# Two transformer blocks on one core: the second block's last 128 tokens begin with their convolutions, the head norms are summed as columns, and the chores are paced by the busier engine

## The reference, cut to what matters

```
x = first_block(...)    # adaLN, sparse attention + short convolution, then a product-key expert layer:
                        #   per token 128 experts; each expert's row of 2048 numbers (u, v) is gathered:
                        #   out = sum_e gelu(x . u_e) * g_e * v_e ;  x + gate * out, final rmsnorm
h = rmsnorm(x);  proj = h @ w_in            # w_in: 1024 x 10256
q_a k_a v_a z_a q_b k_b v_b z_b beta decay gate_a gate_b = split(proj)
o_a = causal attention(rope(q_a), rope(k_a), v_a);   y_a = (o_a * silu(z_a)) @ w_branch_a
q_b k_b v_b = silu(causal conv of 4 taps over tokens)
q_b = q_b * rsqrt(sum_head q_b^2 + eps) * dk^-0.5;   k_b = k_b * rsqrt(sum_head k_b^2 + eps)
o_b = gated delta rule(q_b, k_b, v_b, decay, beta)   # state carried from token to token, 8 heads of 128
y_b = (rmsnorm(o_b) * silu(z_b)) @ w_branch_b
out = (sigmoid(gate_a) * y_a + sigmoid(gate_b) * y_b) @ w_out;   return x + rmsnorm(out)
```

## Time and profile before

| what | us |
|---|---|
| median of 3 runs | 1382.6 (1382.16 to 1389.08) |
| the profiled execution, its own time | 1377.14 |
| its span, first to last instruction | 1375.3 |
| TensorE busy | 1099.7 (80%) |
| VectorE busy | 816.1 (59%) |
| ScalarE busy | 450.3 (33%) |
| GpSimd busy | 288.9 (21%) |
| gathers issued | 213.2 to 1040.1 |
| last accumulate | 1057.2 |

### The profile page before, as it was taken

The page is one execution under the profiler, slowest core; times in us unless marked ns, Lnnn a source line. Parts: engine busy times, 40 slices in busy tenths (PEclk is TensorE's granted clock), DMA queues, the critical chain, the costliest instruction groups (busy, mean ns, idle before and its releaser), DMA issues.

```text
span 1375.3 us, 14070 instructions
## 1 busy us (share of the span) xinstructions
PE 1099.7 (80%) x5130; PEld 545.3 (40%) x5130; DVE 816.1 (59%) x1849; ACT 450.3 (33%) x1246; POOL 288.9 (21%) x261
## 2 busy tenths in 40 slices
PE   6989995877786666678877799875888798798687
PEld 2877672432252222123333343323333354454353
DVE  5475656887946998463456765566553317535531
ACT  1121223555433344352334433433342213113111
POOL 0000002434343535433222232331321000000000
PEclk9987977999998999999999899998989899899798
DMA  9995507999999999999999799997988475156132
GB/s 392 328 388 198 199 0 274 336 353 395 383 384 422 420 405 391 422 421 422 420 422 403 270 420 421 421 421 287 421 331 346 180 276 214 66 212 259 76 123 76
DMA packets 63664, 433.14 MB, mean 315 GB/s; under 512 B 6979, under 2 KB 10348, under 8 KB 11884
## 3 DMA queue, kind: packets, MB, share of 16 engines
q0 software_dynamic: 36864, 268.45, 48.4%
q1 hardware_dynamic: 26064, 161.76, 30.0%
q10 hardware_dynamic: 668, 2.04, 0.4%
HBM read 431.17 MB, written 1.06 MB: 314 GB/s over the span
## 4 chain that ended last, share of the span: by engine, by line
PE 44%; DVE 25%; DMA 21%; ACT 7%; issue 3%; POOL 1%; ACTq 0%; SPq 0%; DVEq 0%; POOLq 0%
DMA AR<-in_puv,idx 18%; PE ps L1055 17%; PE ps L1010 8%; DVE AR L1619 8%; PE ps L704 4%; PE ps L1161 2%; PE ps L926 2%; DMA W<-in_w_mod 2%; PE ps L1036 1%; DVE rowb L1766 1%; PE ps L954 1%; DVE tok L1802 1%; DVE rowb L1802 1%; DMA X<-in_x 1%; ACT av L2128 1%
## 5 line engine op out<-in xcount | busy, mean ns | idle before, releaser
L2377 POOL DMA_INDIRECT AR<-in_puv,idx x256 | 288.5, 1127 | 752.7 <-PE ps L1010 501.5
L1010 PE MATMUL ps<-AR,acc 128*64 128x512 f32 x912 | 288.3, 668 | 124.8 <-ACT acc L2011 123.9
L1619 DVE CUSTOM_DVE_ANT_0 AR<-AR,mixT 128x1024 f32<-128x1024 f32 x128 | 153.3, 1222 | 84.2 <-DMA AR<-in_puv,idx 83.9
L1055 PE MATMUL ps<-W,AR 128*128 128x512 f32 x416 | 197.2, 614 | 3.2 <-ACT AR L2011 2.2
L1010 PEld LDWEIGHTS ps<-AR,acc 128*64 128x64 f32 x912 | 72.2, 146 | 293.3 <-ACT acc L2011 201.5
L1619 DVE CUSTOM_DVE_ANT_0 AR<-AR,tok 128x1024 f32<-128x1024 f32 x128 | 153.2, 1220 | 58.6 <-DMA AR<-in_puv,idx 58.5
L2126 ACT ACTIVATE av<-av 128x1 f32<-128x1 f32 x256 | 51.6, 201 | 353.1 <-DVE av L1619 352.8
L1055 PE MATMUL ps<-W,hT 128*128 128x512 f32 x320 | 155.1, 616 | 6.0 <-ACT rowb L2011 6.0
L1055 PEld LDWEIGHTS ps<-W,AR 128*128 128x128 f32 x416 | 77.6, 197 | 81.5 <-issue 76.0
L1055 PEld LDWEIGHTS ps<-W,hT 128*128 128x128 f32 x320 | 57.5, 194 | 85.5 <-issue 76.8
L704 PE MATMUL ps<-hT,W 128*128 128x256 f32 x320 | 76.8, 403 | 8.7 <-DVE AR L1343 6.1
(11 more groups left out here) (434 smaller groups left out, 1331.0 us busy)
## 6 DMA issues: line engine op xcount, KB each, us to landing
W<-in_w_in SPq DMA_DIRECT2D x90, 1024.0 KB, 9.0
W<-in_w_mod SPq DMA_DIRECT2D x24, 1024.0 KB, 11.1
W<-in_wba SPq DMA_DIRECT2D x8, 1024.0 KB, 8.2
W<-in_wbb SPq DMA_DIRECT2D x8, 1024.0 KB, 8.1
W<-in_wo SPq DMA_DIRECT2D x8, 1024.0 KB, 8.0
W<-in_w_out SPq DMA_DIRECT2D x4, 1024.0 KB, 5.9
...
AR<-in_puv,idx POOLq DMA_INDIRECT x256, 11.1
```

What stands on the lines that cost most here:

```text
L1010: t = mm(of(("E", a, c))[64 * g:64 * g + 64, :], dg_at((2 * p + g) % NDG, late), GB[:, places[g], D + c * 512:D + c * 512 + 512], start=(m ...
L1055: t = mm(b[:, :], src[:, k, :], slab(i)[:, k, :], start=(k == 0), stop=(k == 7))
L1619: ttr(GB[:, n, 0:D], GB[:, n, 0:D], H2[a][g], 1.0, 0.0, MUL, ADD, av[:, a, c:c + 1]).then_inc(*ve.sig("dot", p, g))
L2377: eng.indirect_dma_start(GB[:, n, :], None, puv, bass.IndirectOffsetOnAxis(ap=idx[:, a, c:c + 1], axis=0)).then_inc(*gp.dma(f"g{n}", "gat" ...
```

## The change

1. `ORDER` becomes one list for each half of the tokens. Within a conv group the columns come as v, q, k (`CONV = (2, 0, 1)`). For a = 1 all six conv columns come first, then q and k, v, zb, za, and the gates with the branches; the delta rule's two groups start early and the attention runs between them.
2. The head norm is summed by four matmuls with the squares as weights and one column of ones as data, so its sums are 128x4, one column per head, tokens on partitions. Root and reciprocal run on that. A diagonal of it, times the all-ones matrix, spreads it over the partitions (`l2_spread`).
3. The convolution chore is split into `conv_turn`, `conv_lo` (halo, two taps, one add) and `conv_hi` (two taps, two adds), with its own buffer for the taps (`tapped`); the silu no longer shares it.
4. A chore's cost is the larger of its TensorE and its VectorE time; the steps share the sum over 64. No chore is free.
5. For a = 0 the second halves of the two `bb` projections, the output projection and `finish` (19 chores) are held back until after the loop; two of them go ahead of the last accumulate, the others between the norm chores of a = 1. For a = 1 the first halves of both output slabs go ahead of the last transpose.
6. Buffers and waits are fitted to the new order (`gs`, `zs`, `earlier`).

```diff
-PIECE, HOP, SPREAD = 1.75, 0.9, 65.0
+PE_TIME = {"proj": 1.75, "beta": 1.4, "products": 2.6, "inv_t": 1.8, "norm_h": 1.8}
+VE_TIME = {"x2_norm": 1.3, "x2_out": 1.3, "norm_h": 1.2, "decay": 3.5, "ms": 1.5, "conv_lo": 2.1, "conv_hi": 2.8, "conv_silu": 1.4,
+           "l2_root": 1.6, "l2_spread": 1.4, "za_out": 1.4, "bb_out": 1.4, "dec": 2.1, "products": 2.9, "inv_start": 2.1, "inv_t": 1.7,
+           "gain_out": 1.5}
+def cost(chore):
+    return max(PE_TIME.get(chore[0], 0.9), VE_TIME.get(chore[0], 0.7))
...
+def second_first():
...
+    proj("ba", 1, hops[14:15], hops[15:16], [("new_values", 0)], [("state", 0)])
+    proj((2, 1), 1, [("read_out", 0)])
+    proj((0, 1), 1, [("conv_turn", 2, 1)], [("conv_lo", 2, 1)], [("conv_hi", 2, 1)])
+    proj((1, 1), 1, [("conv_turn", 0, 1), ("conv_silu", 2, 1)], [("conv_lo", 0, 1)], [("conv_hi", 0, 1)])
+    proj("zb", 0, [("conv_turn", 1, 1), ("conv_silu", 0, 1)], [("conv_lo", 1, 1), ("l2_mm", 0, 1), ("conv_hi", 1, 1)], [("conv_silu", 1, 1)])
...
+    proj("bb", 0, hops[10:11], hops[11:12], k1=4)
+    proj("bb", 1, hops[12:13], hops[13:14], k1=4)
+    for hop in hops[14:16] + [("new_values", 1), ("state", 1), ("read_out", 1), ("gain_out", 1), ("ob_turn", 1)]:
+        do(*hop)
+    n = len(c.out)
     proj("bb", 0, k0=4)
     proj("bb", 1, [], [("m_turn", 0)], k0=4)
     proj("o", 0, [], [("m_turn", 1)])
     proj("o", 1)
+    do("finish")
+    return c.out[:n], c.out[n:]
+def second_last():
...
+    c.norm()
+    proj((2, 0), 0, [], [("beta",)])
+    proj((0, 0), 0, [("conv_turn", 2, 0)], [("conv_lo", 2, 0)], [("conv_hi", 2, 0)], [("decay",)])
+    proj((1, 0), 0, [("conv_turn", 0, 0), ("conv_silu", 2, 0)], [("conv_lo", 0, 0)], [("conv_hi", 0, 0)], [("decay_sum",)])
+    proj((2, 1), 1, [("conv_turn", 1, 0)], [("conv_lo", 1, 0), ("conv_silu", 0, 0)], [("conv_hi", 1, 0), ("l2_mm", 0, 0)])
+    proj((0, 1), 1, [("conv_turn", 2, 1), ("conv_silu", 1, 0)], [("conv_lo", 2, 1), ("l2_mm", 1, 0)], [("l2_root", 0), ("conv_hi", 2, 1)], [("l2_spread", 0)])
+    proj((1, 1), 1, [("conv_turn", 0, 1), ("conv_silu", 2, 1)], [("conv_lo", 0, 1)], [("conv_hi", 0, 1)], [("dec", 0)])
+    proj("q", 0, [("conv_turn", 1, 1)], [("conv_silu", 0, 1), ("conv_lo", 1, 1)], [("products", 0)], [("conv_hi", 1, 1), ("l2_mm", 0, 1)])
+    proj("k", 0, [("values", 0)], [("inv_start", 0), ("conv_silu", 1, 1)], [("rope_turn", "q", 0)], [("inv_x", 1, 0), ("l2_mm", 1, 1)])
+    proj("q", 1, [("inv_t", 1, 0), ("l2_root", 1)], [("inv_x", 2, 0)], [("rope_turn", "k", 0), ("inv_t", 2, 0), ("l2_spread", 1)], [("inv_x", 3, 0)])
...
+    proj("zb", 1, [("inv_x", 5, 1), ("gain_out", 0)], [("inv_t", 5, 1), ("mpv", 1)], [("inv_x", 6, 1), ("mt", 2)], [("inv_t", 6, 1), ("ms", 3)])
+    proj("za", 0, [("rest", 1), ("mpv", 2)], [("new_values", 1), ("mt", 3)], [("ob_turn", 0)], [("read_out", 1), ("mpv", 3)])
...
+    proj("bb", 1)
+    proj("o", 0, k1=4)
+    proj("o", 1, [], [("m_turn", 1)], k1=4)
+    proj("o", 0, k0=4)
+    proj("o", 1, k0=4)
...
+    assert not rest
+    last = second_last()
+    for _ in range(2):
+        do(*held.pop(0))
     do("accumulate", *lag)
+    while held:
+        do(*last.pop(0))
+        for _ in range(2):
+            if held:
+                do(*held.pop(0))
+    for chore in last:
+        do(*chore)
...
-                mm(b[:, :], ones, sq[a], start=True, stop=True).then_inc(*pe.sig("l2_mm", a, j, n))
+                for q in range(4):
+                    t = mm(b[:, q:q + 1], sq[a][:, q * P:q * P + P], ones[:, 0:1], start=True, stop=True)
+            def l2_spread(a, n):
+                    b, old = take(("l2s", a, j, n), (("l2_q", "l2_k")[j], a, n))
+                    mm(b[:, :], ones, dgl[a][:, j, :], start=True, stop=True).then_inc(*pe.sig("l2_sp", a, j, n))
...
-            def l2_scale(a, n):
-                    t = link(rec(r, r))
-                    stt(o, o, (0.5 * DK, 0.5)[j], heads(r), MUL, MUL)
+            def l2_root(a, n):
+                t = link(rec(lr[a], lr[a]))
+                for j in range(2):
+                    tt(heads(dgl[a][:, j, :]), ident.unsqueeze(1).to_broadcast([P, 4, P]),
+                       lr[a][:, 4 * j:4 * j + 4].unsqueeze(2).to_broadcast([P, 4, P]), MUL)
+            def l2_spread(a, n):
+                    stt(o, o, (0.5 * DK, 0.5)[j], heads(of("l2s", a, j, n)[:, :]), MUL, MUL)
```

More of the change, by code:

```diff
@@ L66 @@
     "ve_moba": ("m_max", "m_rec", "mPT", "oa"),
-    "ve_conv2": ("tail", "conv2", "silu", "l2_sq", "l2_k", "l2_q"),
+    "ve_conv2": ("tail", "halo1", "conv_lo", "conv2", "silu", "l2_sq", "l2_dg", "l2_k", "l2_q"),
     "ve_delta": ("beta", "dt", "dt_abs", "decay", "G", "dec_min", "dec", "kG", "kdec", "Q", "qd"),
@@ L226, in second_chores @@
     proj("v", 0, [], [("rope_turn", "k", 1)], [("beta",)])
[L227 to L235 removed]
+    proj("v", 1, [("decay",)], [], [("ms", 0)])
@@ L236, in second_chores @@
+    proj((2, 0), 0, [("decay_sum",)], [("mt", 0)], [("ms", 1)], [("mpv", 0)])
+    proj((0, 0), 0, [("conv_turn", 2, 0), ("mt", 1)], [("conv_lo", 2, 0)], [("conv_hi", 2, 0), ("mpv", 1)])
+    proj((1, 0), 0, [("conv_turn", 0, 0), ("conv_silu", 2, 0)], [("conv_lo", 0, 0)], [("conv_hi", 0, 0)])
+    proj("za", 0, [("conv_turn", 1, 0), ("conv_silu", 0, 0)], [("conv_lo", 1, 0), ("l2_mm", 0, 0), ("conv_hi", 1, 0)], [("conv_silu", 1, 0)])
     hops = levels(0)
-    proj("za", 1, two * [("mt", 3)] + hops[0:1], two * [("mpv", 3)] + hops[1:2], hops[2:3], [("oa_turn", 0)])
@@ L253, in second_chores @@
-    proj("bb", 0, hops[12:13], hops[13:14], k1=4)
-    proj("bb", 1, hops[14:15], hops[15:16] + two * [("rest", 1)], k1=4)
-    for name in ("new_values", "read_out") if two else ("new_values", "state", "read_out"):
-        do(name, 1)
-    do("gain_out", 1)
-    do("ob_turn", 1)
+    proj("ba", 1, hops[14:15], hops[15:16], [("new_values", 0)], [("state", 0)])
+    proj((2, 1), 1, [("read_out", 0)])
+    proj((0, 1), 1, [("conv_turn", 2, 1)], [("conv_lo", 2, 1)], [("conv_hi", 2, 1)])
+    proj((1, 1), 1, [("conv_turn", 0, 1), ("conv_silu", 2, 1)], [("conv_lo", 0, 1)], [("conv_hi", 0, 1)])
@@ L262, in second_chores @@
     proj("o", 1)
-    do("finish", cost=0)
-    return out
+    do("finish")
+    return c.out[:n], c.out[n:]
+def second_last():
+    c = Chores(1)
+    do, proj = c.do, c.proj
+    c.norm()
+    proj((2, 0), 0, [], [("beta",)])
[7 more added lines that the diff above has]
+    proj("q", 1, [("inv_t", 1, 0), ("l2_root", 1)], [("inv_x", 2, 0)], [("rope_turn", "k", 0), ("inv_t", 2, 0), ("l2_spread", 1)], [("inv_x", 3, 0)])
+    proj("k", 1, [("inv_t", 3, 0), ("dec", 1)], [("inv_x", 4, 0)], [("rope_turn", "q", 1), ("inv_t", 4, 0)], [("products", 1), ("inv_x", 5, 0)])
+    proj("v", 0, [("inv_t", 5, 0)], [("inv_x", 6, 0), ("values", 1)], [("rope_turn", "k", 1), ("inv_t", 6, 0)], [("inv_start", 1), ("rest", 0)])
+    proj("v", 1, [("inv_x", 1, 1), ("new_values", 0)], [("inv_t", 1, 1), ("ms", 0)], [("inv_x", 2, 1), ("read_out", 0)], [("inv_t", 2, 1), ("mt", 0), ("ms", 1)])
+    proj("zb", 0, [("inv_x", 3, 1)], [("inv_t", 3, 1), ("mpv", 0)], [("inv_x", 4, 1), ("mt", 1)], [("inv_t", 4, 1), ("ms", 2)])
+    proj("zb", 1, [("inv_x", 5, 1), ("gain_out", 0)], [("inv_t", 5, 1), ("mpv", 1)], [("inv_x", 6, 1), ("mt", 2)], [("inv_t", 6, 1), ("ms", 3)])
+    proj("za", 0, [("rest", 1), ("mpv", 2)], [("new_values", 1), ("mt", 3)], [("ob_turn", 0)], [("read_out", 1), ("mpv", 3)])
+    proj("za", 1, [], [("oa_turn", 0), ("gain_out", 1)], [("ob_turn", 1)])
+    proj("ga", 0, [], [], [("oa_turn", 1)])
+    for key, n in (("ba", 0), ("ga", 1), ("ba", 1), ("gb", 0)):
+        proj(key, n)
+    proj("bb", 0)
+    proj("gb", 1, [], [("m_turn", 0)])
+    proj("bb", 1)
[3 more added lines that the diff above has]
+    proj("o", 1, k0=4)
+    do("finish")
+    return c.out
@@ L405, in loop_chores @@
     h1, h2, second, spread = half1(pair), 0, False, 0
-    rest = second_chores(0)
-    share, spent, lag = sum(cost for cost, _ in rest) / SPREAD, 0.0, None
+    rest, held = second_first()
+    share, spent, lag = sum(map(cost, rest)) / 64, 0.0, None
     for p in range(P):
@@ L451, in loop_chores @@
             while rest and spent > 0:
-                cost, chore = rest.pop(0)
-                spent -= cost
+                chore = rest.pop(0)
+                spent -= cost(chore)
                 do(*chore)
+    assert not rest
+    last = second_last()
+    for _ in range(2):
+        do(*held.pop(0))
     do("accumulate", *lag)
-    last = second_chores(1)
-    while rest or last:
+    while held:
+        for _ in range(1):
+            do(*last.pop(0))
         for _ in range(2):
-            if rest:
-                do(*rest.pop(0)[1])
-        if last and (not rest or last[0][1][0][:2] == "x2"):
-            do(*last.pop(0)[1])
+            if held:
+                do(*held.pop(0))
+    for chore in last:
+        do(*chore)
     return out
```

196 lines of the change are left out of this document (105 added, 91 removed).

## The result

| | before | changed | predicted |
|---|---|---|---|
| median of the runs, us | 1385.4 (1382.2 to 1389.1, 4 runs) | 1341.2 (1339.8 to 1346.3, 4 runs) | 1332 (1312 to 1358) |
| the profiled execution, its own time | 1377.1 | 1341.3 | |
| its span | 1375.3 | 1339.4 | |
| accumulate 125 starts | 1043.4 | 1019.6 | 1012.8 |
| last accumulate starts | 1057.2 | 1050.7 | near 1037 |

The ratio is 0.9687 (95% interval 0.9647 to 0.9727): faster, 9 us slower than forecast, inside the range. The spans differ by 35.9 us, the medians by 44.2, because the profiled execution of before was 8.3 us faster than its median and that of the changed kernel lay on it.

The account below looks back on a forecast made before the run. DMA, except in holes, was taken to bound 600 to 1055 us, TensorE the last tokens. Terms -36 + 6 + 8 + 2 - 6.6 - 24 = -50.6 off 1382.6 gave 1332 us, range 1312 to 1358.

Parts of the forecast that it names:

- The last 128 tokens: Reordered last stretch, TensorE-bound: 299.2 us falls to 263, difference -36 (bounds -46 and -15).
- rival B: VectorE bounds the last tokens, with TensorE waiting 26 us more: 1358 us; chance 9%.
- Eight passes with one column: Head norm sums on TensorE: eight one-column passes taken to cost the same as the old 0.86 us matmul, difference 0.
- Until accumulate 125: Loop from 600 us to accumulate 125: filled DMA holes -24 and later weight loads -6.6.
- holes -24: DMA holes in the loop from 600 us: 25.9 us lost, 2 remain, so -24 (bounds 0 and -25.9).
- weights -6.6: Projections finishing later keep slab loads out of the loop: 2.8 MB at 421 GB/s, -6.6 us (0 to -12).
- Rival A: The loop's holes stay because in-order TensorE still holds accumulates back; 20 of 24 us not recovered: 1352 us; chance 12%.
- The end of the loop: Serial end of the inverse in the last two steps: accumulate 127 later, +8 us, plus +2 for half-speed accumulates.
- its sign of being wrong: Prediction wrong if the last accumulate is later than 1047, or VectorE over 90% busy early in the tail with TensorE waiting over 15.
- Held back: Two half slabs of bb and both of o moved behind the loop for tokens 0 to 127: +6 us (+4 to +17).
- Rival C: Slower: the gather buffer ring drains in 28 convolution or norm steps, 78 us lost on top: 1410 us; chance 5%.
- The two rules weighed: Skill rules set aside: a 1.38 us drain per ScalarE table switch (time 1336); HBM limit near 358 GB/s, filling holes gaining nothing.

Follow-up runs that it names:

- Experiments 2: The changed kernel with the old head norm (128x512 sum, root and reciprocals, no spread): 1351.9 us, ratio to the kernel before 0.9786.
- 8: The changed kernel with the pacing costs of before, convolution and root parts mostly free: 1338.4 us, ratio to the kernel before 0.9651.
- 10: The changed kernel with conv_hi directly behind conv_lo for tokens 0 to 127, conv_lo, conv_hi, conv_silu, l2_root and l2_spread costing nothing: 1341.3 us, ratio 0.9691.
- Version 11: The changed kernel with old head norms, unsplit convolution for tokens 0 to 127 and old pacing costs, keeping order and held chores: 1354.6 us, ratio 0.9776.
- experiment 1: The kernel before with only the head norm changed (column sums, 128x8 root and reciprocal, spread), all inside the old l2_scale chore: 1377.0 us, ratio 0.9946.

## Why the prediction was right, and where it was not

The way, the size and the path of most of the gain were right: the loop's holes close and the last tokens run against TensorE. That the time came out only 9 us off is partly luck. The four terms were together 14.7 us too hopeful (6.8, 7.2, 2.0 and -1.3); the profiled execution of before was 8.3 us under its median, and its median rose by 2.8 from the forecast's 1382.6. 14.7 - 8.3 + 2.8 = 9.2.

**The last 128 tokens: -36 forecast, -37.3 measured; right in its parts.** The four longest waits found on paper were the first transpose of the inverse (2.9), the two column sums (1.2 and 1.1) and the first `inv_t` (1.1); measured 2.5, 1.4, 0.9 and, for two hops of the inverse, 1.4 and 1.6. All waits sum to 10.1 us (7.3 forecast); the 2 us for half clock were not needed (0.99). VectorE was busy 71% in the first 60 us (42.3) and 78% from 1100 to 1150, so rival B did not occur. Of the gain the order alone gives 26.5 and the norms on top of it 11.

**Eight passes with one column: taken as even (0.85), measured 1.05 us,** inside the bounds, 0.2 more than the sum that they replace. The small reciprocal took 0.20 (0.17 forecast), the spread 0.86 as forecast. So the sums aren't even for TensorE but cost it 0.2 x 8 = 1.6 us in all.

**Until accumulate 125: -30.6 forecast (holes -24, weights -6.6), -23.8 measured; size off by 6.8.** The holes named did close, but the forecast left 2 us of loss at 421 GB/s, and the stretch ran at 412: 413 x (1 - 412/421) = 8.8 us. Part of it is a shallow new hole at 590 to 630 (share 0.91, 40 x 0.09 = 3.6 us; 1.01 before), where TensorE waits 6.87 us for the norm's VectorE steps ahead of its transposes at 602.38. Counted until the last gather has landed, 1054.9 before and 1022.2 now, the DMA is 32.7 us earlier. From 560 us on it moved 195.0 MB until then before and 190.9 now (windows of 494.9 us at 394 and 462.2 at 413 GB/s), so some 10 of the 32.7 us are weights no longer loaded there and 23 are holes. The weights term was right in kind and within its bounds (0 to -12). The reason that I gave for the holes was wrong in part: I credited less VectorE time per step and the pacing. Experiments 2, 8, 10 and 11 took these away singly and together, and as long as the order stood no deep hole came back and the loop's end lay within 3 us; experiment 1 had the new norms without the order, and the hole stayed. Of the 24 GB/s won from 640 to 1010 us 9 hang on these parts together. Rival A stayed away mainly on account of a part of the change that my argument for this term hardly used.

**The end of the loop: +8 and +2 forecast, +17.2 measured; the step that failed.** Its chain was drawn rightly, but I priced its hops at full clock and left only 2 us for half clock on the accumulates. The granted clock was 0.68. Against my prices the two inverse hops lost 0.9 and 1.2, new values 1.2, the accumulate 1.6, the transposes 0.4 and the two pieces 2.8: 8.1 us, 6.1 more than allowed. Version 11 runs the same three hops at full clock:

```profile
1031.42 1.13 PE L1226 MATMUL ps<-RT,hT 128*128 128x128 f32 x8 [1.46 <-DVE RT L1959]
1033.24 1.16 PE L1226 MATMUL ps<-RT,PT 128*128 128x128 f32 x8 [0.69 <-ACT PT L2341]
1035.18 1.16 PE L1249 MATMUL ps<-hT,RT 128*128 128x128 f32 x8 [0.78 <-DVE RT L1959]
```

They take 1.13 to 1.16 where I had 0.89 and 0.9, the price of a group with others right ahead of it. So 0.8 of the 8.1 us was my price and 7.3 the clock. Version 11, with only the transposes and the two pieces slow, takes 26.8 us from 125 to 127; the changed kernel takes 31.1, and I had 24.0. Of these 7.1 us 5.3 are clock beyond the 2 allowed and 0.8 price; the other 1.0 has its nearest cause in pair 126: its second dot waited 1.24 us for its gather and stood ahead of the correction of the inverse on VectorE. The last accumulate came at 1050.7, past the 1047 that the prediction had set as its sign of being wrong, and by that sign it was wrong here. The range, of 20 and 26 us to its sides, was wide enough for the miss, and the last tokens, 1.3 us better than forecast, gave a little back.

**Held back: +6 forecast, +8.0 measured.** The cover held; the 2 us are TensorE's wait of 3.00 at 1059.68 for the copy of a transposed output, which stood behind the norm's squares on ScalarE.

**Rival C** did not occur: between 640 and 1010 us no window of 20 us has a DMA share under 0.97.

**The two rules weighed.** ScalarE's table load at 1039.39 took 1.28 us and the root began at 1040.68, so the trace shows no drain behind a switch of set. The Trainium skill, "ScalarE: Activation LUTs", section "What ACT_TABLE_LOAD costs", adds 1.38 us; by that rule the excess of the loop's end would have been partly a drain, and the rows say it was not. The DMA moved 421 GB/s in full stretches and 412 over 413 us, and filling the holes brought the last gather in some 23 of its 33 us earlier (above). The Trainium skill, "DMA: Bandwidth & Descriptors", section "Where 436 GB/s comes from", has HBM bind near 358 GB/s; that limit was not seen here.
